# Head sums of a query/key norm as two rounded parts, in a two-block transformer kernel

## The reference

```python
def rms_norm(x, g):
    xf = x.astype(jnp.float32)
    y = xf * lax.rsqrt(jnp.mean(xf * xf, axis=-1, keepdims=True) + EPS)
    return (y * g.astype(jnp.float32)).astype(x.dtype)
...
    nq = rms_norm(na[:, :, 0], g_nq)
    nk = rms_norm(na[:, :, 1], g_nk)
```

## Time and profile before

| | us |
|---|---|
| median of 3 runs | 1900.99 |
| lowest, highest | 1900.92, 1901.82 |
| the profiled execution, its own time | 1900.59 |
| its span in the trace | 1898.6 |
| TensorE matmul busy | 1855.3 |
| VectorE busy | 1354.4 |
| ScalarE busy | 927.9 |
| mean granted TensorE clock, share of full | 0.997 |

### The profile page before, as it was taken

One profiled execution on the slowest core, in us unless ns is written; L12 is line 12 of the kernel. 1 busy time (PEld: TensorE's weight loads), 2 busy tenths in 40 slices (PEclk: granted clock), 3 DMA queues, 4 the chain that ended last, 5 costly groups with the idle time before them and its releaser, 6 DMA issues.

```text
span 1898.6 us, 29221 instructions
## 1 busy us (share of the span) xinstructions
PE 1855.3 (98%) x11256; PEld 1566.6 (83%) x11256; DVE 1354.4 (71%) x2488; ACT 927.9 (49%) x1695; POOL 28.3 (1%) x57
## 2 busy tenths in 40 slices
PE   8999999999999999999999999999999999999998
PEld 4777556788888888888776899999999889999986
DVE  6665776688898888866477777666776675776674
ACT  3345565553533232335556665545454564554563
POOL 0000000000000000000000000000000000000000
PEclk9999999999999999999999999999999999999999
DMA  7332301254355545414232355555454335454323
GB/s 302 114 124 71 128 23 67 90 166 167 110 223 189 210 178 199 178 67 132 71 117 95 112 181 216 178 181 184 158 164 154 116 100 167 158 166 156 122 91 122
DMA packets 55576, 272.74 MB, mean 144 GB/s; under 512 B 6416, under 2 KB 6544, under 8 KB 38288
## 3 DMA queue, kind: packets, MB, share of 16 engines
q1 hardware_dynamic: 47808, 225.40, 34.4%
q0 software_dynamic: 7632, 45.47, 6.8%
HBM read 269.79 MB, written 1.05 MB: 143 GB/s over the span
## 4 chain that ended last, share of the span: by engine, by line
PE 83%; DVE 10%; ACT 4%; issue 2%; DMA 1%; SPq 0%; ACTq 0%; DVEq 0%
PE bank L608 20%; PE bank L610 19%; PE bank L609 19%; DVE small_lo L2113 3%; PE bank L966 2%; PE bank L644 2%; PE bank L974 2%; PE bank L766 2%; PE bank L1071 1%; PE bank L656 1%; ACT small_hi L1539 1%; DVE wide L2728 1%; DVE w_parts L2100 1%; PE bank L713 1%; PE bank L711 1%
## 5 line engine op out<-in xcount | busy, mean ns | idle before, releaser
L608 PE MATMUL bank<-h_hi,small_hi 128*128 128x256 f32 (+3 forms) x992 | 309.6, 312 | 3.6 <-DVE h_lo L2243 1.4
L610 PE MATMUL bank<-h_hi,small_lo 128*128 128x256 f32 (+3 forms) x992 | 299.8, 302 | 0.0
L609 PE MATMUL bank<-h_lo,small_hi 128*128 128x256 f32 (+3 forms) x992 | 298.5, 301 | 0.0
L2113 DVE TENSOR_TENSOR small_lo<-ring,small_hi 128x1024 fp32r<-128x1024 f32 (+1 forms) x192 | 226.7, 1193 | 99.4 <-ACT small_hi L1539 98.4
L1524 ACT ACTIVATE w_parts<-ring 128x1024 fp32r<-128x1024 f32 x192 | 201.2, 1051 | 163.5 <-PE bank L610 163.5
L609 PE MATMUL bank<-h_parts,w_parts 128*128 128x256 f32 (+1 forms) x784 | 260.0, 332 | 0.0
L2100 DVE TENSOR_TENSOR w_parts<-ring,w_parts 128x1024 fp32r<-128x1024 f32 x192 | 233.1, 1218 | 21.0 <-ACT w_parts L1524 20.9
L609 PE MATMUL bank<-b_parts,w_parts 128*128 128x256 f32 (+1 forms) x656 | 217.1, 331 | 0.0
L1539 ACT ACTIVATE small_hi<-ring 128x1024 fp32r<-128x1024 f32 (+1 forms) x192 | 193.4, 1026 | 31.1 <-PE bank L1288 15.9
L608 PEld LDWEIGHTS bank<-h_hi,small_hi 128*128 128x128 f32 (+2 forms) x992 | 185.5, 187 | 17.2 <-issue 5.6
L609 PEld LDWEIGHTS bank<-h_lo,small_hi 128*128 128x128 f32 (+2 forms) x992 | 184.4, 186 | 10.7 <-issue 2.2
(11 more groups left out here) (329 smaller groups left out, 3891.7 us busy)
## 6 DMA issues: line engine op xcount, KB each, us to landing
ring<-in_w SPq DMA_DIRECT2D x204, 512.0 KB, 3.5
ring<-in_w SPq DMA_DIRECT2D x96, 1024.0 KB, 4.8
lowrank<-in_rows POOLq DMA_DIRECT2D x24, 1024.0 KB, 5.1
prob<-in_rows POOLq DMA_DIRECT2D x24, 512.0 KB, 3.9
wide<-in_ada SPq DMA_DIRECT2D x8, 1024.0 KB, 9.9
ring<-in_w SPq DMA_DIRECT2D x14, 384.0 KB, 3.3
lowrank<-in_bias POOLq DMA_DIRECT2D x2, 2048.0 KB, 10.8
x<-in_x SPq DMA_DIRECT2D x2, 1024.0 KB, 9.9
```

What stands on the lines that cost most here:

```text
L608: pe.matmul(ps, w[0][:, k, :], hi, start=k == 0, stop=False)
L609: pe.matmul(ps, w[0][:, k, :], lo, start=False, stop=False)
L610: return pe.matmul(ps, w[1][:, k, :], hi, start=False, stop=k == nk - 1)
L2113: dve.tensor_tensor(small_lo[:, slot, 0:size], small[:, slot, 0:size], small_hi[:, pair, 0:size].bitcast(F32), ALU.subtract).then_inc(*sig ...
```

## The change

For the query and key tiles 0 and 1 of both layers, and the query tiles 2 and 3 of layer 1, ScalarE rounds the square into a second buffer of the ring, VectorE subtracts it from the square in place, and TensorE adds two products of rounded operands. The matrix `pair`, exact in rounded form, leaves the constants that are loaded; VectorE writes it from blocks of `ones` at the start, and TensorE waits for it. `two_sums` says which tiles.

```diff
-CONST, NCONST = columns([("ident", P), ("ones", P), ("pair", P), ("rot", P), ("half", 2), ("eps", 1), ("one", 1),
+CONST, NCONST = columns([("ident", P), ("ones", P), ("rot", P), ("half", 2), ("eps", 1), ("one", 1),
...
+        def square_part(key):
+            return sq_r[:, numbers.get(("slot", "sq", key), 0), :]
+
+        def two_sums(name, i, l):
+
+            return name in ("nq", "nk") and (i < 2 or (name == "nq" and l == 1))
...
+        pair_at = -(-nc.sbuf_base // 32) * 32
+        sb("pair", [P, P])
...
+        sq_r = part("sq_r", [P, 4, TT], sq_at)
+        pair_r = part("pair_r", [P, P], pair_at)
...
+        pair = pair_r[:, :].bitcast(F32)
...
             def head_sum(name, i, l, w, among=None):
 
+                if two_sums(name, i, l):
+                    ps = next_bank("ss", (name, i), l, until=("rs_log", (name, i), l), among=among)
+                    pe.wait_ge(*event("square_hi", (name, i), l))
+                    pe.matmul(ps[:, 0:w], pair_r[:, :], square_part(((name, i), l, 1))[:, 0:w], start=True, stop=False)
+                    pe.wait_ge(*event("square_lo", (name, i), l))
+                    mm = pe.matmul(ps[:, 0:w], pair_r[:, :], square_part(((name, i), l, 0))[:, 0:w], start=False, stop=True)
+                    return full(mm, "ss", (name, i), l)
                 if name in ("nq", "nk"):
...
             pe.wait_ge(*event("con_in"))
+            pe.wait_ge(*event("pair_r"))
...
                         square(*key, heads1[name][:, i, c0:TT])
+                    if two_sums(name, i, l):
+                        take(act, "sq", ((name, i), l, 1), ("psum_full", "ss", (name, i), l))
+                        act.wait_ge(*event("squared", (name, i), l, 0))
+                        act.activation(square_part(((name, i), l, 1))[:, 0:TT - c0], given("sq", ((name, i), l, 0))[:, 0:TT - c0],
+                                       ACT.Copy).then_inc(*signal("square_hi", (name, i), l))
...
             dve.wait_ge(*event("con_in"))
+            for a in range(2):
+                for b in range(2):
+                    rows, cols = slice(ND * a, ND * a + ND), slice(ND * b, ND * b + ND)
+                    ins = dve.tensor_scalar(pair_r[rows, cols], ones[rows, cols], float(a == b), None, ALU.mult)
+            ins.then_inc(*signal("pair_r"))
...
+                def low_square(name, i, w):
+
+                    dve.wait_ge(*event("square_hi", (name, i), l))
+                    dve.tensor_tensor(square_part(((name, i), l, 0))[:, 0:w], given("sq", ((name, i), l, 0))[:, 0:w],
+                                      square_part(((name, i), l, 1))[:, 0:w].bitcast(F32),
+                                      ALU.subtract).then_inc(*signal("square_lo", (name, i), l))
...
                         if i and not (behind and i == 4):
                             scale_head(name, i - 1, c0)
+                        if two_sums(name, i, l) and i < 4:
+                            low_square(name, i, TT - c0)
                         if i == 1 and behind:
                             behind()
```

More of the change, by code:

```diff
@@ L337, in program @@
         x = sb("x", [P, KT, TT])
+        sq_at = -(-nc.sbuf_base // 32) * 32
         sq_all = sb("sq", [P, 4, TT])
+        assert nc.sbuf_base == sq_at + 4 * 4 * TT
         rs_at = -(-nc.sbuf_base // 32) * 32
@@ L437, in c @@
             return con[:, CONST[name][0]:CONST[name][1]]
-        ident, ones, pair, eps, one = c("ident"), c("ones"), c("pair"), c("eps"), c("one")
+        ident, ones, eps, one = c("ident"), c("ones"), c("eps"), c("one")
+        pair = pair_r[:, :].bitcast(F32)
         cq = lowrank[:, 0:3072].rearrange("p (k t) -> p k t", k=6)
@@ L3052, in constants @@
     put(con, CONST, "ones", 1.0)
-    put(con, CONST, "pair", (i[:, None] // 64 == i[None, :] // 64))
     rot = np.zeros((ROPE, ROPE))
```

## The result

The change made the kernel slower by a little: 1903.34 us, the median of 12 runs (1901.26 to 1905.59), against 1900.55 for 12 runs of before (1899.60 to 1901.82). The ratio is 1.0017, with a 95% interval of 1.0009 to 1.0024. That is within the 0.2% the prediction named as its resolution, and outside its range (1898.8 to 1902.8). Its upper end, 1.0024, is a little over 0.2%. The profiled execution took 1905.02, with a span of 1903.2.

What follows compares the result with a forecast made beforehand. TensorE, busy for 98% of the span, was taken as the bound. Layer 0 +0.7, layer 1 +0.1 - 0.8 and start -0.15 sum to about -0.15 us, so 1900.8 was predicted, range 1898.8 to 1902.8.

Steps and rivals of the forecast that it cites:

- The sums on TensorE: Ten head sums as rounded pairs: gain 0.40 per wide and 0.19 per narrow sum, 3.2 us if nothing waits.
- Rival D: The rounded pair runs no faster than the full product, so layer 1's 0.8 + 0.8 are lost: 1902.4; chance 0.04.
- The lag in layer 0: At tile 1, ScalarE's rounding copy (0.66) and VectorE's subtraction (0.60) make the next tile's copy begin 1.26 later.
- Rival A: VectorE has missed slack, so up to all of 3.2 + 0.15 is won: 1897.6 to 1899.7; chance 0.14.
- Layer 0 as a whole: +0.7: Layer 0's queries +0.07, and its last key sum starts 0.7 later: +0.7 instead of -1.6.
- Layer 1, query tile 2: TensorE waits for VectorE's subtraction; second product starts about 883.5, done at 883.6; step forecast +0.66.
- Layer 1's keys: Idle of 1.26 ahead of tile 2's copy just takes the shift; two wide sums keep their gain: -0.8.
- The start: Four scalings delay first products up to 0.8, covered by ScalarE's 2.51 idle; smaller con lands x earlier: -0.15.
- Rival C: The moved start shifts the low-clock stretch at 25 to 32 us: 1898 without it, 1902.4 if longer; chance 0.05.
- Rival B: TensorE waits for the subtraction at nine of ten tiles, 0.95 each: +5.4, 1906.4; chance 0.09.
- weaker form: Waits for the subtraction only at the four narrow tiles, plus a longer lag in layer 0: +1.5, 1902.5.

Runs made afterwards that it cites:

- layer0_only: The change with only layer 0's sums split (query and key tiles 0 and 1), layer 1 as before: 1904.09 us, ratio 1.0018 against before.
- filled: The whole change plus five useless TensorE products ahead of layer 0's last query sum and last key sum: 1901.16 us, ratio 1.0006 against before.
- before_lag2: The kernel before, no rounded sums, with three useless VectorE reductions behind scale_head of key tile 0, layer 0: 1904.33 us, ratio 1.0018 against before.
- layer1_only: The change with only layer 1's sums split (four query tiles, key tiles 0 and 1): 1899.78 us, ratio 0.9998 against before.
- chosen_early: The change with layer 0 split only at tile 0 of queries and keys, and layer 1's query tile 2 subtracted ahead of the weight split: 1898.68 us, ratio 0.9993.
- before_lag: The kernel before, no rounded sums, with three useless VectorE reductions ahead of low_cq(1) in layer 0's keys: 1900.27 us, ratio 1.0003 against before.
- pair_only: The kernel before with only the pair matrix written on the chip by VectorE, no sum split: 1899.96 us, ratio 1.0000 against before.
- low_first: The whole change with VectorE's subtraction (low_square) moved ahead of scale_head of the tile before: 1898.96 us, ratio 0.9996 against before.

## Why the prediction was wrong

**The sums on TensorE: right.** 0.40 for a wide sum and 0.19 for a narrow one were forecast; the steps of the first two tiles are 0.40 to 0.42 each in layer 0 and in layer 1's keys, and 0.19 to 0.25 in layer 1's queries. Rival D is out. The Trainium skill (TensorE: Matmul & The Clock Gate, Back-to-back issue gap) has 131 ns for such products; the trace has 240, and the measurement decides. (By the page's figure a wide sum would have gained 0.60, not the 0.59 of the prediction.)

**The lag in layer 0: right.** Taking off the 0.98 with which after enters the layer, the copy of query tile 3 begins at 120.1 (forecast 120.0), that of key tile 2 at 141.9 (141.8), that of key tile 3 at 147.1 (147.0), and the last key sum at 148.6 (148.3 to 148.5). All in all the queries cost +0.12 and the keys +0.66, where +0.07 and +0.63 were forecast. Rival A is out: nothing of the gain was kept in layer 0. The Trainium skill (TensorE: Matmul & The Clock Gate, Architectural detail) calls the queues of VectorE and ScalarE strict first-in, first-out; the trace agrees, since the copies wait behind row products that they have nothing to do with.

**The step that failed: "Layer 0 as a whole: +0.7".** It prices TensorE's standing still at its length. The last key sum waited 2.16 rather than 0.68, and behind it the granted clock fell to 0.50 for 6.8 us, which added 3.25. The prediction read the earlier trace rows, where the clock is low at the start, and gave a rival to the clock there alone; the wait itself follows from its numbers (0.68 + 0.7 + the 0.8 that TensorE arrives earlier = 2.2), but it did not ask what the clock does behind it. layer0_only has the drop and loses 3.26 by it, filled has the wait partly covered and no drop, and before_lag2 has the wait without the change, and the loss by its median. So the chain is shown: VectorE's lag, TensorE stands still for 2.2, the clock falls in the profiled executions of after and layer0_only, and 3.3 more are lost. What is not shown is why it did not fall there in the profiled execution of before_lag2.

**Layer 1, query tile 2: the second term that was mis-sized.** Forecast +0.66, measured +1.32. Here is VectorE's timeline of after at tile 2, answering to the earlier trace rows:

```profile
884.03 2.46 DVE L2080 SCALAR_TENSOR_TENSOR lowrank<-lowrank,par,rs 128x256 f32<-128x256 f32 x6
886.41 1.21 DVE L2140 TENSOR_TENSOR small_lo<-ring,small_hi 128x1024 fp32r<-128x1024 f32 x1
887.54 0.47 DVE L2080 SCALAR_TENSOR_TENSOR wide<-wide,gq,rs 128x256 f32<-128x256 f32 x1
887.94 0.41 DVE L2396 TENSOR_TENSOR sq_r<-sq,sq_r 128x256 fp32r<-128x256 f32 x1
```

With the entry shift of 4.92 taken off, the subtraction starts at 883.02 and TensorE's second product at 883.49, both exactly as forecast. What failed is "is done at 883.6": the product behind it starts not 0.12 but 0.62 later (888.41 to 889.03), and the one after that 0.31 later rather than 0.23. These 0.50 and 0.08 are nearly all of what 1.32 has over 0.66. layer1_only repeats them: a wait of 0.77, then 0.62 and 0.31. What holds the product behind the released one is not shown; the view has 0.23 of idle time there with no releaser, and the weight split that chosen_early waits for was done here at 887.62.

**Layer 1's keys: right**, -0.83 for -0.8: the idle of 1.26 did take the lag.

**The start: a cost of 0.4 that the prediction had covered, and a scatter that is not the change's.** The second squares of x began at 22.45, inside the 22.3 to 22.5 forecast, and the scalings took 0.60. But the cover was read on ScalarE alone, and the path goes on through VectorE's row products. The timeline of VectorE, before and then after:

```profile
27.37 0.08 DVE L2167 DVE_READ_ACCUMULATOR probT<-wide,c_rows 128x1 f32 x1
27.56 1.23 DVE L2167 SCALAR_TENSOR_TENSOR probT<-wide,c_rows 128x1024 f32<-128x1024 f32 x1
```

```profile
27.32 0.08 DVE L2199 DVE_READ_ACCUMULATOR probT<-wide,c_rows 128x1 f32 x1
27.92 1.23 DVE L2199 SCALAR_TENSOR_TENSOR probT<-wide,c_rows 128x1024 f32<-128x1024 f32 x1 [0.51 <-DVE probT L2199]
```

The distance is 0.19 with the old start (before, before_lag, before_lag2) and 0.58 to 0.60 in all ten kernels with the new one. What holds it is open: the releaser that the view names is VectorE's own earlier product, long done. It reaches TensorE: from the second squares to the first projection product are 14.83 in before_lag and before_lag2 and 15.24 in all ten, whether their clock fell on the way or not. So the new start costs 0.4 where 0.15 was to be won. In before the same distance is 15.56, since its clock was at half from 24.62 to 31.44, and that hid the 0.4 in pair_only's shift.

The rest of after's +0.98 is the clock. after was 0.37 ahead of before at the first projection, and then fell to half from 37.23 to 40.65, on the projections themselves. layer1_only, whose start is the same code as pair_only's, fell from 37.65 to 41.06, while pair_only fell from 25.41 to 28.82 and filled not at all. With the start unchanged, before_lag arrived 0.98 earlier than before did. So this stretch varies by about 1 us from execution to execution. Rival C put this scatter down to the change.

**Rival B** (a wait for every subtraction) is out: one wait of 0.77 and no other. Its weaker form (1902.5) and rivals C and D (1902.4) came nearest to the median of 1903.34, and that is luck: none of them has the clock falling behind a standstill.

**The sum, against the median.** Forecast -0.15; with the two steps that failed, 3.25 and 0.66 more, it is +3.8, and with the start's +0.98 in place of its -0.15 it is +4.9. The spans of the profiled pair differ by 4.6, their times by 4.4. The medians have +2.8. Five of after's twelve runs took 1901.26 to 1902.39 and seven 1903.25 to 1905.59, a pattern like that of before_lag2's runs. The mean granted clock on record is 0.998 in all of the five and 0.997 in all of the seven, so the slower ones had more low clock. That it fell behind the sum in them is argued, since only one of after's executions has a profile.

## What to carry to other kernels

Where TensorE is the bound and an in-order engine feeds it, price an added operation on that engine by what stands *behind* it, up to the next consumer that is late, and look for idle *ahead* of a wait to put it in: there the same 0.6 (or 2.1, with the slacks behind it) cost TensorE nothing. Check then what the move pushes back in its turn: in chosen_early it was the weight split. Price a new standstill of TensorE at more than its length: here one of 0.77 cost 0.6 more behind it, and one of 2.2 cost 3.3 more through the clock in two profiled executions and nothing in a third. And split only where nobody is made late: seven chosen tiles did better than all ten as first placed. All ten with the subtraction moved (low_first) lie as low by their median, but still have the drop of the clock in their profile.

## What was unexpected of the hardware

**The clock behind a standstill.** It fell behind one of 2.16 (after) and 2.15 (layer0_only) for 6.8 us, at a cost of 3.3; behind one of 1.56 (low_first) for 3.4 us, at 1.7; and not behind one of 1.63 (after, at 122.56), nor in the profiled execution behind one of 2.17 (before_lag2). In after and layer0_only it fell 0.3 and 0.2 us into the sum that ended the wait, in low_first 1.9 us behind that sum's start, among the products that follow it. So the length of the gap alone does not tell; what else decides stays open.

**A second weak place.** In before_lag2 and chosen_early the clock fell near 230 us as well, where before kept 1.00 (and so did after). The windows of before_lag2, then of before:

```profile
228.00:235.00 7.00, 5.59 (x19) 3.32 (x19) 5.83 (x16) 5.78 (x13) 0.00 (x0) 0.76 1.02 435
```

```profile
228.00:235.00 7.00, 5.38 (x28) 2.93 (x30) 6.17 (x16) 6.63 (x16) 0.00 (x0) 1.00 0.99 421
```

TensorE's busy time is 5.6 or less of the 7.0 us in both, and the drop (0.76 on average here) cost 0.7. No part of either edit lies there.

**The restart.** After the wait of 0.77 TensorE started its next product 0.62 behind the released one, where a product of that width otherwise takes 0.12. layer1_only shows the same 0.62, and low_first 0.53 behind a released product that came only 0.2 late. Why is open.
